# Latent attention with its values one unit later, and three smaller edits to a two-layer encoder kernel

## What is computed

```python
# latent attention of layer 1, 8 heads, scale = (64 + 32) ** -0.5
s = (einsum('bqhd,bkhd->bhqk', qn, k_nope) + einsum('bqhr,bkr->bhqk', qp, k_pe)) * scale
p = softmax(s, axis=-1)
o = einsum('bhqk,bkhd->bqhd', p, v)
# memory keys and values: kv = mem @ w_kv
# every norm: (x - mu) * rsqrt(var + eps) * g + b
# experts: top-1 group, top-2 experts in it; out = sum of gate * (silu(x @ w_gate) * (x @ w_up)) @ w_down
```

## Time and profile before

| | |
|---|---|
| runs | 2414.78, 2418.31, 2420.05 us; median 2418.31 |
| profiled execution | 2414.21 us, of it the span 2411.9 |
| busy share of the span | PE 91%, PE weight loads 48%, DVE 33%, ACT 19%, POOL 14% |
| granted clock of PE | mean 0.957 |

### The profile page before, as it was taken

One profiled execution on the slowest core, in us unless ns is written; L12 is line 12 of the kernel. 1 busy time (PEld: TensorE's weight loads), 2 busy tenths in 40 slices (PEclk: granted clock), 3 DMA queues, 4 the chain that ended last, 5 costly groups with the idle time before them and its releaser, 6 DMA issues. The chain is left out here.

```text
span 2411.9 us, 38329 instructions
## 1 busy us (share of the span) xinstructions
PE 2192.0 (91%) x15591; PEld 1169.7 (48%) x15591; DVE 797.4 (33%) x1779; ACT 457.8 (19%) x927; POOL 344.1 (14%) x401
## 2 busy tenths in 40 slices
PE   8999998886999999999698999899699999999964
PEld 4665757553444444444444555565444444444422
DVE  1133333634212121121815665542431212121216
ACT  0030304221101010011224444331200101010101
POOL 0000000141111111113600000004211111111305
PEclk9999998986999999999899999999699999999997
DMA  9013103444999999997510000011479999999945
GB/s 354 2 58 117 40 1 118 158 159 159 389 393 387 391 382 390 382 390 299 183 54 37 1 1 1 15 57 44 193 270 386 392 389 393 381 384 393 370 158 209
DMA packets 97064, 535.53 MB, mean 222 GB/s; under 512 B 20784, under 2 KB 44624, under 8 KB 72016
## 3 DMA queue, kind: packets, MB, share of 16 engines
q1 hardware_dynamic: 78864, 492.32, 52.5%
q0 software_dynamic: 18112, 41.99, 4.9%
HBM read 511.21 MB, written 41.45 MB: 229 GB/s over the span
## 5 line engine op out<-in xcount | busy, mean ns | idle before, releaser
L827 PE MATMUL banks<-ring,arena 128*32 128x256 f32 (+3 forms) x9952 | 1300.5, 461 | 41.9 <-DMA ring<-in_exp_w_gu 17.2
L827 PEld LDWEIGHTS banks<-ring,arena 128*32 128x32 f32 (+2 forms) x9952 | 537.9, 123 | 745.7 <-issue 607.8
L827 PE MATMUL banks<-ring 128*128 128x512 f32 (+3 forms) x1232 | 339.9, 550 | 5.6 <-issue 4.0
L827 PEld LDWEIGHTS banks<-ring 128*128 128x128 f32 (+2 forms) x1232 | 168.5, 188 | 149.4 <-issue 138.8
L1835 DVE TENSOR_TENSOR arena<-arena,banks 128x384 f32<-128x384 f32 x65 | 36.0, 555 | 614.0 <-ACT arena L1398 604.2
L827 PE MATMUL banks<-arena 128*64 128x128 f32 (+5 forms) x1664 | 155.4, 299 | 36.2 <-DVE recip_t L2019 20.4
L763 POOL DMA_INDIRECT expert_out<-arena,scatter_idx x64 | 61.3, 958 | 828.7 <-DVE arena L1844 808.3
L1398 ACT ACTIVATE arena<-banks 128x384 f32<-128x384 f32 x65 | 31.9, 491 | 739.7 <-PE banks L827 739.7
L827 PEld LDWEIGHTS banks<-arena 128*64 128x64 f32 (+3 forms) x1664 | 136.8, 165 | 60.9 <-ACT arena L1494 26.2
L720 POOL TENSOR_TENSOR arena<-arena,ln_gb 128x1024 f32<-128x1024 f32 x28 | 69.5, 2484 | 598.1 <-ACT arena L1363 598.1
L1841 DVE COPY arena<-banks 32x256 f32<-32x256 f32 x132 | 56.2, 425 | 280.0 <-PE banks L827 279.1
(11 more groups left out here) (179 smaller groups left out, 1524.6 us busy)
## 6 DMA issues: line engine op xcount, KB each, us to landing
ring<-in_exp_w_gu SPq DMA_DIRECT2D x130, 2048.0 KB, 17.7
ring<-in_exp_w_down SPq DMA_DIRECT2D x65, 2048.0 KB, 23.0
ring<-in_x_t SPq DMA_DIRECT2D x6, 2304.0 KB, 16.2
moe_in<-arena POOLq DMA_DIRECT2D x16, 512.0 KB, 3.0
arena<-expert_out SPq DMA_DIRECT2D x16, 512.0 KB, 4.4
ring<-expert_out SPq DMA_DIRECT2D x16, 512.0 KB, 5.5
ring<-in_a_w_in SPq DMA_DIRECT2D x6, 1024.0 KB, 17.5
arena<-in_a_w_in SPq DMA_DIRECT2D x4, 1024.0 KB, 13.5
```

The costliest lines, as they stand in the source:

```text
L827: return nc.tensor.matmul(out, lhsT, rhs, start=start, stop=stop)
```

## The change

The values of a unit are formed during the next one, with a second buffer for the transposed exponentials where the output weights lay, so that these are loaded later. The maximum comes out negated and unscaled; the scale goes into the queries: into ACT's copy of the unrotated part, and as its square root into the rotary table, which both the queries and the keys are multiplied with. The first loads are cut into two halves along the contraction, and so are the key products. In norm 3 the additions of tiles 1, 3 and 5 go from POOL to DVE, three tiles behind. The factor -mean/std is computed with another instruction. Half of the overflow pass's last copies go to ACT.

```diff
+        probs_turned = [prob_t, ring_at(64, 2, S)]
...
+        SHIFT_ON_DVE = (1, 3, 5)
         def wait_tokens(eng, i, t):
-            if t < TT - 1:
+            if i == 3 and t in SHIFT_ON_DVE:
+                eng.wait_ge(x_shifted, SHIFT_ON_DVE.index(t) + 1)
+            elif i == 3 and t < TT - 1:
+                eng.wait_ge(x_ready, i * (TT - 1) + t + 1 - sum(o < t for o in SHIFT_ON_DVE))
+            elif t < TT - 1:
...
 # SP, mem_loads
-                sp.dma_start(mem_t[l], ...).then_inc(mem_in, 16)
-                sp.dma_start(mem_w[l][:, :, 0:GW], w[:, :, 0:GW]).then_inc(mem_in, 16)
+                for ks, landed in ((slice(0, KT // 2), mem_in), (slice(KT // 2, KT), mem_rest_in)):
+                    sp.dma_start(mem_t[l][:, ks], ...).then_inc(landed, 16)
+                    sp.dma_start(mem_w[l][:, ks, 0:GW], w[:, ks, 0:GW]).then_inc(landed, 16)
 # SP, expert_phase
                 if l == 1:
                     sp.wait_ge(pv, unit0[(1, "mem")])
+                    sp.dma_start(w_out[1], ...).then_inc(wout_in, 16)
 # SP, main program, ahead of expert_phase(1)
-            sp.dma_start(w_out[1], ...).then_inc(wout_in, 16)
 # POOL, norm_scale
-                        pool.wait_ge(gmul_done, n)
-                        nc.gpsimd.tensor_tensor(X[:, t], X[:, t], ln_gb[:, 1], ALU.add).then_inc(x_ready, 1)
+                        if not (i == 3 and t in SHIFT_ON_DVE):
+                            pool.wait_ge(gmul_done, n)
+                            nc.gpsimd.tensor_tensor(X[:, t], X[:, t], ln_gb[:, 1], ALU.add).then_inc(x_ready, 1)
 # PE, mem_projection
-                pe.wait_ge(mem_in, 32 * (l + 1))
-                for j in range(2):
-                    for k in range(KT):
-                        mm(ps[:, 6, j * MEM:(j + 1) * MEM], ...)
+                for half, landed in enumerate((mem_in, mem_rest_in)):
+                    pe.wait_ge(landed, 32 * (l + 1))
+                    for j in range(2):
+                        for k in range(4 * half, 4 * half + 4):
+                            mm(ps[:, 5 + j, 0:MEM], ...)
 # PE, group_projection
                 pe.wait_ge(wv_in[b], 16 * uses)
+                pe.wait_ge(mem_kv_act, 1)
 # PE, latent_attention: values read probs_turned[u % 2]
                 for u in range(PAIR_UNITS):
+                    if u > 0:
+                        reciprocals(u - 1)
                     if more:
                         score(u + 1)
                     turn(u, 1)
-                    reciprocals(u)
                     ...                       # pair_projection(m + 1, t)
-                    values(u)
+                    if u > 0:
+                        values(u - 1)
                     if more:
                         turn(u + 1, 0)
+                reciprocals(PAIR_UNITS - 1)
+                values(PAIR_UNITS - 1)
 # ACT, experts: overflow pass
+                for b in range(2):
+                    act.wait_ge(ys_out[b], 16 * 16 * (l + 1))
...
                         silu().then_inc(o["silu"], 1)
+                        act.wait_ge(o["pe_steps"], 4 * j + 4)
+                        for g in range(2):
+                            nc.scalar.copy(ys[WIDE:CAP, 0, g * 256:(g + 1) * 256], ps[NARROW * g:NARROW * g + NARROW, 7, 0:256])
+                        nc.scalar.copy(ys[0:WIDE, 0, 0:HALF], ps[0:WIDE, 6]).then_inc(o["y_act"], 1)
 # ACT, pair_copy and exponentials
-                nc.scalar.copy(dst, proj_bank(m, i)).then_inc(head_act, 1)
+                nc.scalar.activation(dst, proj_bank(m, i), ACT.Copy, scale=1.0 if i % 3 == 2 else SCALE_B).then_inc(head_act, 1)
-                                         bias=neg_max[:, hd, 0:1], scale=SCALE_B, accum_out=stat[:, hd, 1, 0:1]).then_inc(probs, 1)
+                                         bias=neg_max[:, hd, 0:1], accum_out=stat[:, hd, 1, 0:1]).then_inc(probs, 1)
 # ACT and DVE, turned
-                    wait_ge(pv, u0 + 2 * u)
+                    wait_ge(pv, u0 + 2 * max(u - 1, 0))
 # DVE, tile_rstd
-                nc.vector.scalar_tensor_tensor(out=rstd[:, t, 1:2], in0=mean_var[:, t, 0:1], scalar=-1.0, in1=rstd[:, t, 0:1],
-                                               op0=ALU.mult, op1=ALU.mult).then_inc(rs_done, 1)
+                nc.vector.tensor_scalar(rstd[:, t, 1:2], mean_var[:, t, 0:1], rstd[:, t, 0:1], -1.0, ALU.mult, ALU.mult).then_inc(rs_done, 1)
 # DVE, overflow pass
-                        for g in range(4):
+                        for g in range(2, 4):
                             narrow_out(0, g)
-                        wide_out(0, 0)
                         wide_out(0, 1).then_inc(o["dve_steps"], 1)
 # DVE, combine, after last_scale
+                    if l == 1 and t - 3 in SHIFT_ON_DVE:
+                        dve.wait_ge(gmul_done, i * (TT - 1) + t - 2)
+                        nc.vector.tensor_tensor(X[:, t - 3], X[:, t - 3], ln_gb[:, 1], ALU.add).then_inc(x_shifted, 1)
 # DVE, maximum
-                    V.tensor_reduce(stat[:, hd, 0, 0:1], ..., AX.X, ALU.max).then_inc(row_max, 1)
-                    dve.wait_ge(row_max, n + 1)
-                    V.tensor_scalar(neg_max[:, hd, 0:1], stat[:, hd, 0, 0:1], -SCALE_B, None, ALU.mult).then_inc(max_ready, 1)
+                    V.tensor_reduce(neg_max[:, hd, 0:1], ..., AX.X, ALU.max, negate=True).then_inc(max_ready, 1)
 # DVE, latent_attention
                 for u in range(PAIR_UNITS):
+                    if u > 0:
+                        keep_reciprocals(u - 1)
...
                     if more:
                         maximum(u + 1, 0)
+                        maximum(u + 1, 1)
                     turned(u, 1)
-                    dve.wait_ge(recip_ps, u + 1)
-                    V.tensor_copy(recip_t[:], ps[:, 6, P:2 * P]).then_inc(recip_kept, 1)
+                    if u > 0:
+                        normalise(u - 1)
                     if more:
-                        maximum(u + 1, 1)
+                        turned(u + 1, 0)
                     if m + 1 < MLA_H // 2 and t in (0, 3):
                         pair_rope(m + 1, t // 3)
-                    dve.wait_ge(pv, u0 + 2 * u + 2)
-                    V.tensor_tensor(mla_t[:, m, t * P:(t + 1) * P], ps[:, 6, 0:P], recip_t[:], ALU.mult).then_inc(o_out, 2)
-                    if more:
-                        turned(u + 1, 0)
+                keep_reciprocals(PAIR_UNITS - 1)
+                normalise(PAIR_UNITS - 1)
 # constants
-        "rope_b": rope_table(ROPE_B, ROPE_B, 4, np.arange(S)),
+        "rope_b": np.float32(SCALE_B ** 0.5) * rope_table(ROPE_B, ROPE_B, 4, np.arange(S)),
```

More of the change, by code:

```diff
@@ L308, in build @@
         ov = [{n: sem(f"ov{l}_{n}") for n in
-               ("w_in", "slots", "idx", "xs", "pe_steps", "silu", "dve_steps", "out")}
+               ("w_in", "slots", "idx", "xs", "pe_steps", "silu", "dve_steps", "y_act", "out")}
               for l in range(DEPTH)]
@@ L1238, in values @@
                             h = 2 * m + hd
-                            last = mm(ps[DH * hd:DH * hd + DH, 6, 0:P], v_b[:, c, h * DH:(h + 1) * DH], prob_t[:, hd, c * P:(c + 1) * P], c == 0, c == TT - 1)
+                            last = mm(ps[DH * hd:DH * hd + DH, 6, 0:P], v_b[:, c, h * DH:(h + 1) * DH], probs_turned[u % 2][:, hd, c * P:(c + 1) * P], c == 0, c == TT - 1)
                     last.then_inc(pv, 2)
@@ L1303, in mem_keys @@
                 act.wait_ge(mem_proj, l + 1)
-                nc.scalar.copy(km_t[:], ps[:, 6].rearrange("p (a b) -> p a b", a=2)).then_inc(mem_kv_act, 1)
+                nc.scalar.copy(km_t[:], ps[:, 5:7, 0:MEM]).then_inc(mem_kv_act, 1)
             def group_values(g):
@@ L1492, in turned @@
                     act.wait_ge(probs_t, u0 + n + 1)
-                    act.wait_ge(pv, u0 + 2 * u)
-                    nc.scalar.copy(prob_t[:, hd, 0:HALF], ps[:, 4]).then_inc(pt_act, 1)
+                    act.wait_ge(pv, u0 + 2 * max(u - 1, 0))
+                    nc.scalar.copy(probs_turned[u % 2][:, hd, 0:HALF], ps[:, 4]).then_inc(pt_act, 1)
                 exponentials(0, 0)
@@ L1995, in maximum, with keep_reciprocals, normalise @@
                     dve.wait_ge(scores, u0 + n + 1)
-                    V.tensor_reduce(stat[:, hd, 0, 0:1], ps[:, 2 * hd:2 * hd + 2].rearrange("p a b -> p (a b)"), AX.X, ALU.max).then_inc(row_max, 1)
-                    dve.wait_ge(row_max, n + 1)
-                    V.tensor_scalar(neg_max[:, hd, 0:1], stat[:, hd, 0, 0:1], -SCALE_B, None, ALU.mult).then_inc(max_ready, 1)
+                    V.tensor_reduce(neg_max[:, hd, 0:1], ps[:, 2 * hd:2 * hd + 2].rearrange("p a b -> p (a b)"), AX.X, ALU.max,
+                                    negate=True).then_inc(max_ready, 1)
                 def turned(u, hd):
                     dve.wait_ge(probs_t, u0 + 2 * u + hd + 1)
-                    dve.wait_ge(pv, u0 + 2 * u)
-                    V.tensor_copy(prob_t[:, hd, HALF:], ps[:, 5]).then_inc(pt_dve, 1)
+                    dve.wait_ge(pv, u0 + 2 * max(u - 1, 0))
```

(8 more changed lines are left out.)

10 lines of the change are left out of this document (7 added, 3 removed).

## The result

The changed kernel takes 2386.9 us (median of 2381.8, 2386.9, 2387.0 and 2387.0), the kernel before 2416.6 in the same session. The ratio of all runs is 0.9868, 95% interval 0.9855 to 0.9882; that of the two medians alone is 0.9877. The forecast was 2392, with a range of 2385 to 2403: the direction was right, the time came out 5 us lower, and the gain was 29.6 us by the medians and 31.9 by the ratio where 26.3 was forecast. The profiled execution took 2381.76 us, of it the span 2379.9; the one before 2414.21 and 2411.9. So the two traces differ by 32.0 us where the sum had 25.95.

A forecast was written before the change was run, and what follows sets the result against it. TensorE was busiest, its longest single-cause wait on VectorE's copy of the reciprocals; -15.9 - 2.9 - 3.55 - 1.5 - 2.1 = -25.95 from 2414.2 gives 2388, set to 2392 for the median; range 2385 to 2403.

The forecast's parts named there:

- tail term: Norm 3 at the end: three additions moved to DVE end the adds 3.4 earlier, one more store costs 1.3; net -2.1.
- latent attention: Values a unit later leave DVE's chain: units without a projection 7.36 instead of 8.39, key units 7.91, query 8.76; -15.9.
- first loads: Start of the kernel: PE can start at 6.8, when the first half of the loads is in; -2.9.
- overflow pass: The one overflow pass: half of DVE's last copies, 3.12 us on the path, go to ScalarE; -1.5.
- fall of the granted clock: Latent stage: sign that the forecast is wrong, if the granted clock of 1.00 (2.4 GHz) falls there.
- output weights, loaded late: Load issued near 1564, landing within 10 us, wanted by PE 40 us later; no wait, no cost.
- Factor: Norms: the replacing operation takes 0.16 even beside busy POOL; combine of layer 0 and output projection of layer 1, -3.55.
- The first rival: POOL still holds the norms' factor: the -3.55 go, the tail is +4.3 instead of -2.1; 2402 us, chance 0.10.
- norm 2: Last tile of layer 1's output projection: the factor falls from 1.42 to 0.16 with everything after waiting; -1.25.
- combine: Combine of layer 0: a hold of 0.45 in each tile goes, about 5 tiles gain; -2.3.
- Slower: Latent attention: the negated maximum takes d longer than the plain one, costing 62d - 12; rival, chance 0.03.

The follow-up runs named there:

- run 1: The kernel before with the latent part of the change alone: 0.9935 of the kernel before, which is 15.7 us.
- run 2: The kernel before with the halved first loads alone: 0.9987 of the kernel before, 3.1 us.
- run 4: The changed kernel with all additions of norm 3 back on POOL: 0.9915 of the kernel before, 8.4 us behind the changed kernel.
- run 5: The changed kernel with the norms' factor computed by the two-tensor operation as before: 0.9908 of the kernel before, 4.3 us behind the changed kernel.
- run 10: The changed kernel with one memset on POOL behind a wait for all eight stores: 0.9911 of the kernel before, span 2390.07 us.
- run 7: The changed kernel with a second, unused reduction ahead of each maximum: 1.0154 of the kernel before, 68 us behind the changed kernel.

## Why the prediction was right in the main, and which step failed

The step that failed is the tail term, -2.1 where -5.6 was measured: it took the landing of the last store as the end of the program, and the end followed POOL's last operation. The latent attention, the first loads and the overflow pass came about as laid out. That the time came within 5 us of the forecast is in part luck: the tail's 3.5 too many and 6 us by which the trace of before was slow in untouched stretches stand, in the profiled pair, against some 5 us lost elsewhere.

**Latent attention** (-15.9; -17.2 where the clock held). The mechanism is as put down: units of 7.30 (7.36), 7.90 (7.91) and 8.76 (8.76), the wait moved ahead of the transposes, the end 8.1 from the first transposes of the last unit to the end of its values (8.0). Of the 1.3 between -15.9 and -17.2, the 0.06 too many in a unit makes 0.8; one unit of before had taken 8.74 and not the 8.39 of all others, which gives 0.3; and the first two distances from scores to scores went from 7.11 to 6.74 and from 8.76 to 7.29, 1.8 together where 1.6 was put down. The maximum with its sign took 1.22, as before. The fall of the granted clock that I named as a thing that would make the forecast wrong did happen in the profiled execution (windows: us, busy time and count of PE, PEld, DVE, ACT, POOL, then clock, DMA share and GB/s):

```profile
1280.00:1284.00 4.00, 1.56 (x12) 0.31 (x8) 2.35 (x2) 1.15 (x3) 0.00 (x0) 0.92 0.00 0
1284.00:1288.00 4.00, 3.89 (x14) 2.54 (x16) 0.99 (x3) 1.77 (x4) 0.00 (x0) 0.50 0.00 0
1288.00:1292.00 4.00, 4.00 (x23) 1.74 (x20) 0.89 (x1) 0.00 (x0) 0.00 (x0) 0.73 0.00 0
```

Behind PE's idle 2.55 us the clock went to 0.50, its lower level of 1.2 GHz, and the transposes took 1.97 instead of 1.09. The stage was 2.8 us longer for it than in run 1. The new code is not needed for this: run 2, with the latent part of before, fell in the same place (its latent stage was 2.6 longer), and runs 1, 4, 5 and 10, with the new one, did not. Whether the change makes it more frequent, one of three profiles without it and five of nine with it, these few can't tell.

The output weights, loaded late, cost nothing: SP issued the load at 1541.05 and PE never waited for it, as costed.

**First loads** (-2.9; -4.1 in the pair, -3.0 in the mean). Right: PE started at 6.36 where I had 6.8. That the 64 products took 15.94 in the pair's second trace and 16.74 in its first is chance (run 2).

**Factor** (-3.55; -1.3 to -2.7 ahead of the tail). The value was right: 0.212 to 0.215 in all 32 places, never held, 0.05 more than the 0.16 that I took. The first rival fell. By the section on interference that it rested on, tensor_scalar could have contended. The same section of the Trainium skill, page "SBUF — State Buffer", Who interferes with whom, says that an operation of DVE with at most one SBUF input outside the two-port modes does not contend with GpSimd. The 32 rows agree with that, for one element a partition; that this instruction, with its scalar in SBUF, counts as one of that kind is not shown otherwise. Two uses of the value were mis-sized. In norm 2 I took the row of before, 1.42, as the price whatever the clock; with the router at the lower level it was 0.38, and 0.1 was gained instead of 1.25. In combine a factor went from 0.60 to 0.21, so 5 tiles would give 1.9, and 1.2 to 1.7 came instead of 2.3; how many tiles PE's work covers is not shown.

**Overflow** (-1.5; -1.5). As put down: from the silu to the store 11.90 became 10.41.

**Tail** (-2.1; -5.6). This is the step that failed. The sum followed the additions to the landing of the stores and took that for the end of the program. The end is the later of that landing and POOL's DRAIN (run 10), and the DRAIN was the later by 3.8 before and by 0.25 in the changed kernel. POOL's last operation ends 5.57 earlier, and the span with it. SP's wait for the stores is over 2.0 earlier against the start of the tail, so the 2.1 was right for a path that did not count, and that by two errors which cancel. A turn of DVE beside POOL costs POOL less than the 1.15 counted: three of POOL's eleven operations take 3.2 instead of 2.35, so 0.86 each, and the additions end 4.45 earlier, not 3.4. And from the last addition to the end of SP's wait there are 5.5 instead of 3.1, so the stores cost 2.4 and not 1.3. Nor is the tail a sum over the edits: without the factor the additions on DVE bring the last addition nothing, without them the factor costs 1. The rival's price for a held factor, the additions 2.6 later than before, was too high: they came 0.3 later.

**Slower** (0.03). Excluded by the 1.22 of the maximum; its price of 62d - 12 held within a tenth in run 7 (68 for 64).

Of the 6 us by which the traces differ from the sum, 3.5 come from the tail, 1.2 from the first loads and 3.3 plus 2.7 from stretches that the change leaves alone (experts of layer 0, memory attention), where the trace of before was on the long side; 1.5 was lost in the latent stage, 0.9 in combine, 1.2 in norm 2 and 1.1 in the rest. The forecast was set 4.1 above the sum for the median of before. The changed kernel's median lies 5.2 above its profiled run, so the offset came out about right; nothing in the sum gave a reason for it, and that is luck too.

## What to carry to other kernels

Lay out one unit of a software pipeline from the durations in the trace: it gave this unit to 0.06 us, and said that delaying one consumer pays until the next wait, which is 0.2 away. Price two edits that share an engine or a port together, not line by line. And find out what ends the program before trimming what comes last: here it was the later of POOL's DRAIN and the wait for the stores. Earlier stores alone gave nothing, and a shorter program on POOL pays only until the stores are the later.

## Unexpected on the hardware

- **POOL's closing DRAIN lasts 7.9 us beyond its last operation.** In 13 of 14 profiles the span ends 8.15 to 8.17 us after that operation, while from DVE's last it is 3.5 to 15.1. The fourteenth is run 5, 9.16, where the wait for the stores set the end. DVE's DRAIN ends 0.05 after its last operation. Why POOL's is so long, no run here shows. The Trainium skill, page "Runtime: NRT & Kernel Launch", section The ~15µs preamble/postamble breakdown, gives stages behind the kernel of 1.5, 1.5 and 2 us for all engines; it names none that is longer for one. No run here shows those stages; the 7.9 us lie inside the span.
- **The granted clock falls or holds behind the same idle 2.5 to 2.8 us of PE.** Six of twelve profiles each way, in kernels with either latent part; a fall cost 1.5 to 2.9 us. A stage's length from one trace carries that much chance.
- **Two edits that undo each other.** The factor alone ends POOL 0.96 later: DVE reaches tile 7 earlier, and two of POOL's operations take 3.3 and 3.2 beside its two turns, where before only the last one took 3.2.
